# Expert blocks: Silu in place of Sigmoid and a product, the bias row spread one block ahead, and the first bias banks written earlier

## The reference, cut to what matters

```
logits = (hf @ router_w + router_b)
top_logits, top_idx = lax.top_k(logits, TOP_K)
gates = jax.nn.softmax(top_logits, axis=-1)
...
def expert_block(args):
    xb, e = args
    gu = xb @ w_gate_up[e] + b_gate_up[e]
    gate, up = jnp.split(gu, 2, axis=-1)
    gate = jnp.minimum(gate, SWIGLU_LIMIT)
    up = jnp.clip(up, -SWIGLU_LIMIT, SWIGLU_LIMIT)
    act = (up + 1.0) * gate * jax.nn.sigmoid(SWIGLU_ALPHA * gate)
    return act @ w_down[e] + b_down[e]
...
y_sorted = yb.reshape(n_rows, d)[dest] * gate_sorted[:, None]
out = jnp.zeros((n, d), h.dtype).at[tok_sorted].add(y_sorted)
```

## Time and profile before

| | us |
|---|---|
| median of 3 runs | 2066.52 |
| the 3 runs | 2066.52, 2068.47, 2065.49 |
| span of the profiled execution, first to last instruction | 2064.2 |
| granted TensorE clock, mean over the span | 0.997 of full speed |
| PE busy | 2018.9 (98%) |
| DVE busy | 1539.6 (75%) |
| ACT busy | 1189.2 (58%) |
| POOL busy | 494.7 (24%) |
| bytes moved by DMA | 521.92 MB |

### The profile page before, as it was taken

The page is one execution under the profiler, slowest core; times in us unless marked ns, Lnnn a source line. Parts: engine busy times, 40 slices in busy tenths (PEclk is TensorE's granted clock), DMA queues, the critical chain, the costliest instruction groups (busy, mean ns, idle before and its releaser), DMA issues.

```text
span 2064.2 us, 26261 instructions
## 1 busy us (share of the span) xinstructions
PE 2018.9 (98%) x9156; PEld 1601.7 (78%) x9156; DVE 1539.6 (75%) x1433; ACT 1189.2 (58%) x1182; POOL 494.7 (24%) x246
## 2 busy tenths in 40 slices
PE   8999999999999999999999999989999999999998
PEld 4865478888888888888888888858888878888887
DVE  5987499999999999999999999985684443333333
ACT  3132277878787878787878788854115632221222
POOL 0005325353434343434343434300000000000000
PEclk9999999999999999999999999999999999999999
DMA  6232599999999999999999999941131213222321
GB/s 228 92 143 89 207 394 407 392 397 378 392 381 391 382 389 380 385 377 390 382 386 386 385 385 383 386 150 69 63 107 70 82 41 113 102 102 83 121 82 41
DMA packets 79078, 521.92 MB, mean 253 GB/s; under 512 B 10368, under 2 KB 10896, under 8 KB 22160
## 3 DMA queue, kind: packets, MB, share of 16 engines
q1 hardware_dynamic: 66560, 484.14, 59.1%
q0 software_dynamic: 8912, 29.57, 5.7%
q10 hardware_dynamic: 3552, 7.46, 1.1%
HBM read 500.53 MB, written 18.60 MB: 251 GB/s over the span
## 4 chain that ended last, share of the span: by engine, by line
PE 84%; issue 5%; POOL 4%; DVE 3%; ACT 2%; DMA 2%; SPq 0%; POOLq 0%; DVEq 0%; ACTq 0%
PE bank L1141 24%; PE bank L1143 23%; PE bank L1142 23%; PE bank L1133 4%; POOL room L600 3%; PE bank L1482 1%; PE bank L1150 1%; ACT bank L842 1%; PE bank L1290 1%; DMA ring<-in_wmoe 1%; PE bank L1330 1%; PE bank L1179 1%; PE bank L1561 1%; PE bank L1542 1%; PE bank L1577 1%
## 5 line engine op out<-in xcount | busy, mean ns | idle before, releaser
L1897 DVE TENSOR_TENSOR ring_r<-ring,room_r 128x2048 fp32r<-128x2048 f32 x384 | 862.5, 2286 | 80.4 <-ACT room_r L774 80.4
L774 ACT ACTIVATE room_r<-ring 128x2048 fp32r<-128x2048 f32 x384 | 724.2, 1911 | 39.3 <-PE bank L1143 34.8
L1142 PE MATMUL bank<-ring_r,room_r 128*128 128x512 f32 x1744 | 679.2, 389 | 0.0
L1141 PE MATMUL bank<-room_r 128*128 128x512 f32 x1576 | 628.9, 399 | 15.8 <-ACT bank L842 13.0
L1143 PE MATMUL bank<-room_r 128*128 128x512 f32 x1568 | 611.8, 390 | 0.0
L1142 PEld LDWEIGHTS bank<-ring_r,room_r 128*128 128x128 f32 x1744 | 327.9, 188 | 66.9 <-issue 3.1
L1141 PEld LDWEIGHTS bank<-room_r 128*128 128x128 f32 x1576 | 295.9, 188 | 88.5 <-issue 29.2
L1143 PEld LDWEIGHTS bank<-room_r 128*128 128x128 f32 x1568 | 294.3, 188 | 63.0
L1141 PE MATMUL bank<-room_r,ring_r 128*128 128x512 f32 x520 | 203.5, 391 | 1.8 <-DVE ring_r L2059 0.9
L1143 PE MATMUL bank<-room_r,ring_r 128*128 128x512 f32 x512 | 199.3, 389 | 0.0
L604 POOL COPY idx_row<-places 96x1 uint32 (+1 forms) x32 | 106.9, 3340 | 267.3 <-DMA sum_rows<-room,idx_row 267.3
(11 more groups left out here) (292 smaller groups left out, 2290.0 us busy)
## 6 DMA issues: line engine op xcount, KB each, us to landing
ring<-in_wmoe SPq DMA_DIRECT2D x384, 1024.0 KB, 10.7
ring<-in_wf SPq DMA_DIRECT2D x33, 1024.0 KB, 4.8
ring<-in_wd SPq DMA_DIRECT2D x7, 2048.0 KB, 9.4
ring<-in_wp SPq DMA_DIRECT2D x14, 1024.0 KB, 4.8
ring<-in_wo SPq DMA_DIRECT2D x2, 2048.0 KB, 8.7
ring<-in_wd SPq DMA_DIRECT2D x2, 1024.0 KB, 9.3
room<-in_xtok ACTq DMA_DIRECT2D x1, 2048.0 KB, 12.6
h_rows<-room POOLq DMA_DIRECT2D x4, 512.0 KB, 3.0
```

Source lines behind the costliest of these rows:

```text
L774: act.activation(w_hi[pair(first, s_)], raw_w[ORDER[s_]], ACT.Copy)\
L1141: pe.matmul(out, x_hi, w_hi, start=start, stop=False, skip_group_check=True)
L1142: pe.matmul(out, x_hi, w_lo, start=False, stop=False, skip_group_check=True)
L1897: dve.tensor_tensor(w_lo[i], raw_w[i], w_hi[pair(first, s_)].bitcast(F32), ALU.subtract)\
```

## The change

Three edits in the expert part. First, ACT computes Silu of 1.702 times the gate bank and DVE's product L1952 is gone; the limit is scaled by 1.702, and the gates that the rows carry are multiplied by 1/1.702 once, before the loop. Second, the bias row of block b + 1 is loaded during the loads of block b (behind piece 3, or behind the last piece for block 0), and POOL spreads it in `block_pool(b)` when the gathered rows of block b + 1 have landed, ahead of the output of block b - 1. POOL then waits for the end of the broadcast, and the broadcast waits until both pairs of bias banks of block b are written. Third, ACT writes the first pair of bias banks straight behind the split of the rows and ahead of the split of the piece of step 1; they wait for the first activation of the block before (`act_ready`), no longer for `x_lo`. A later user of the same memory, in the second model block, gets a wait for the last broadcast.

```diff
-TOP_GATE = float(LIMIT / (1.0 + np.exp(-SW_ALPHA * LIMIT)))
+TOP_SILU = float(SW_ALPHA * LIMIT / (1.0 + np.exp(-SW_ALPHA * LIMIT)))
...
             def block_loads(b, first):
                 expert = sp.value_load(meta[0:1, bass.ts(b, 1)], min_val=0, max_val=E - 1)
-                if not first:
-                    sp.wait_ge(s["bias_spread"], b)
-                sp.dma_start(bias_row, a["bgu"][bass.ts(expert, 1), :]).then_inc(s["bias_in"], 16)
+                if first:
+                    sp.dma_start(bias_row, a["bgu"][bass.ts(expert, 1), :]).then_inc(s["bias_in"], 16)
                 for i in range(PIECES):
...
                     sp.dma_start(raw_w[i], a["wmoe"][bass.ts(expert, 1), i].rearrange("o p n -> (o p) n"))\
                       .then_inc(raw_in[i], 16)
+                    if i == (PIECES - 1 if first else 3):
+
+                        following = sp.value_load(meta[0:1, bass.ds(b + 1, 1)], min_val=0, max_val=E - 1)
+                        sp.wait_ge(s["bias_spread"], b + 1)
+                        sp.dma_start(bias_row, a["bgu"][bass.ts(following, 1), :]).then_inc(s["bias_in"], 16)
...
-            def spread_bias(b, first):
+            def spread_bias(b, first=False):
 
                 wait_counted("bias_in", b * 16 + 16)
                 if not first:
                     wait_counted("seeded", b * CHUNKS)
                 pool.partition_broadcast(bias_wide, bias_row).then_inc(s["bias_spread"], 1)
+                wait_counted("bias_spread", b + 1)
...
                 wait_counted("rows_in", b * 16 + 16)
-                if not first:
-                    spread_bias(b, first)
                 wait_counted("xt_ready", b + 1)
                 gather(b + 1)
+
+                wait_counted("rows_in", b * 16 + 32)
+                spread_bias(b + 1)
                 if not first:
                     rows_out(b - 1)
...
-            def sigmoids(b, c):
+            def silus(b, c):
 
                 act.wait_ge(s["gate_done"], b * CHUNKS + (c + 1))
-                act.activation(sig_sb[0:CAP, :], bank[2 * c][0:CAP, :], ACT.Sigmoid, scale=SW_ALPHA)\
-                   .then_inc(s["sig_done"], 1)
+                act.activation(silu_sb[0:CAP, :], bank[2 * c][0:CAP, :], ACT.Silu, scale=SW_ALPHA)\
+                   .then_inc(s["silu_done"], 1)
...
-                        act.wait_ge(s["x_lo"], b + 1)
+                        act.wait_ge(s["act_ready"], b * CHUNKS - 1)
...
                 split_hi(b, 0)
-                sigmoids(b - 1, 1)
+                silus(b - 1, 1)
                 gathered_hi(b)
+                seeds(b, 0)
                 split_hi(b, 1)
-                seeds(b, 0)
                 split_hi(b, 2)
...
-            step.mark(dve.tensor_copy(pairs[:, :].bitcast(F32).rearrange("p (i k o) -> p i k o", i=TT, k=TOPK)[:, :, :, 2],
-                                      gate[:, :, :]))
+            step.mark(dve.tensor_scalar(pairs[:, :].bitcast(F32).rearrange("p (i k o) -> p i k o", i=TT, k=TOPK)[:, :, :, 2],
+                                        gate[:, :, :], 1.0 / SW_ALPHA, None, ALU.mult))
...
                 own.mark(dve.tensor_scalar(up, bank[2 * c + 1][0:CAP, :], 1.0 - LIMIT, 1.0 + LIMIT, ALU.max, ALU.min))
-                dve.wait_ge(s["sig_done"], b * CHUNKS + (c + 1))
-                own(dve.tensor_tensor(sig, bank[2 * c][0:CAP, :], sig, ALU.mult))
-                dve.scalar_tensor_tensor(act_sb[c][0:CAP, :], sig, TOP_GATE, up, ALU.min, ALU.mult)\
+                dve.wait_ge(s["silu_done"], b * CHUNKS + (c + 1))
+                own.wait()
+                dve.scalar_tensor_tensor(act_sb[c][0:CAP, :], silu_sb[0:CAP, :], TOP_SILU, up, ALU.min, ALU.mult)\
                    .then_inc(s["act_ready"], 1)
...
             step.mark(dve.memset(AT, 0.0))
+
+            dve.wait_ge(s["bias_spread"], T + 1)
             for j in range(4):
```

More of the change, by code:

```diff
@@ L258, in build @@
         up_sb = v(5120, 512)
-        sig_sb = v(5632, 512)
+        silu_sb = v(5632, 512)
         act_sb = [v(6144, 512), v(6656, 512)]
@@ L361, in build @@
             idx_kept tok_kept rows_in bias_in bias_spread seeded hi_done lo_done used gate_done
-            sig_done act_ready xt_ready x_hi x_lo turned act_hi act_lo y_copied row_sel_ready sums_ready c2_in s2_ready x2_ready ss_ready
+            silu_done act_ready xt_ready x_hi x_lo turned act_hi act_lo y_copied row_sel_ready sums_ready c2_in s2_ready x2_ready ss_ready
             un_ready unT_ready uT_done_a uT_done_v p_ready p_evac hsig_ready rot_done fK_ready lv_ready lv_upd
@@ L854, in first_chunk @@
             def first_chunk(b, first=False):
-                sigmoids(b, 0)
+                silus(b, 0)
                 split_hi(b, 9, first)
@@ L890, in rest_act @@
             def rest_act(b):
-                sigmoids(last, 1)
+                silus(last, 1)
                 split_hi(b, 2, end=last)
@@ L1945, in activations @@
             def activations(b, c):
-                own = Steps(dve, s["moe_dve"], b * (2 * CHUNKS) + 2 * c)
-                up, sig = up_sb[0:CAP, :], sig_sb[0:CAP, :]
+                own = Steps(dve, s["moe_dve"], b * CHUNKS + c)
+                up = up_sb[0:CAP, :]
                 dve.wait_ge(s["used"], after(b, 5 + 4 * c))
                 own.mark(dve.tensor_scalar(up, bank[2 * c + 1][0:CAP, :], 1.0 - LIMIT, 1.0 + LIMIT, ALU.max, ALU.min))
-                dve.wait_ge(s["sig_done"], b * CHUNKS + (c + 1))
-                own(dve.tensor_tensor(sig, bank[2 * c][0:CAP, :], sig, ALU.mult))
-                dve.scalar_tensor_tensor(act_sb[c][0:CAP, :], sig, TOP_GATE, up, ALU.min, ALU.mult)\
+                dve.wait_ge(s["silu_done"], b * CHUNKS + (c + 1))
+                own.wait()
+                dve.scalar_tensor_tensor(act_sb[c][0:CAP, :], silu_sb[0:CAP, :], TOP_SILU, up, ALU.min, ALU.mult)\
                    .then_inc(s["act_ready"], 1)
```

## The result

The change makes the kernel slower by 0.5%, little but clear of noise: 2076.72 us (median of 4 runs, 2076.30 to 2076.79) against 2066.39 us for the kernel before, measured beside it (4 runs, 2065.49 to 2068.47). The ratio is 1.0049, 95% interval 1.0035 to 1.0064. The prediction was 2054.8, faster, range 2047 to 2070: wrong in direction, and outside its range. The rival that ended on the other side gave 2074.9.

A forecast was written before the change was run, and what follows sets the result against it. The prediction took PE to bound the kernel, with DVE close behind. Its terms, -17.1 - 1.6 + 1.0 + 3.0 + 3.0 = -11.7 us, gave a span of 2052.5 and a median of 2054.8, range 2047 to 2070.

The forecast's parts named there:

- The rival that ended on the other side: Broadcast let in between DVE's third and fourth splits in every block, +0.3 us a block, 2074.9 us; chance 0.15.
- it misses the gap: Broadcast too late for the pause before DVE's splits of steps 4 to 8: 0.1 us a block, +3.0; chance 0.55.
- The seam's -17.1: PE's lost time between row transposes and step 0 disappears: -0.57 us in each of blocks 2 to 31.
- Worth 0 by itself: Removing DVE's product L1952, 0.68 us twice a block, gains nothing, since PE does not wait for it in the loop.
- I take the upper end: Gathered rows land 10.5 us after the gather starts, from 8.5 to 10.5, so the broadcast is ready at about 883.4.
- It waits for the end of the run: Broadcast waits until DVE's splits of steps 4 to 8 end at 894.6, then holds DVE until 896.5.
- each keeps itself up: Catching or missing the pause before DVE's fourth split repeats from block to block; a late output delays the next gather.
- the 2047.8 of the sum: Time in us if the broadcast hardly holds DVE and the output also keeps its time; hardly held had chance 0.15.
- the 1.89: The time in us for which a broadcast on POOL holds DVE off, out of its 2.29.
- The late output at the end: After the last block, an output 6 to 7 us later makes PE wait for the sums: +3.0, bounds 2 and 5.
- the slower case: Broadcast let in before DVE's fourth split in every block: +0.3 us a block, block 1 adds -0.6; chance 0.15.
- The slower rival: Broadcast delays DVE's fourth split: 0.87 us lost for 0.57 gained a block, period 35.1, 2074.9 us; chance 0.15.

The follow-up runs named there:

- The two runs with the product in one half block: Kernel before with Silu, DVE's product put back in one half block only: first half 2065.43 us, second half 2049.38 us.
- the run behind step 4: Changed kernel with one more POOL wait, for ACT's split of step 4, ahead of the broadcast: 2083.55 us, ratio 1.0082.
- the run behind the activation: Changed kernel with the broadcast also waiting for DVE's activation of the first half of block b: 2053.70 us, ratio 0.9938.
- The mixed row: Changed kernel, spread row holding half of block b + 1's bias and half of block b's, spread ahead of the gather: 2048.47 us; with sigmoid and product 2054.78.

## Why the prediction was wrong

**The step that failed is "it misses the gap", the term of +3.0 (0.1 a block).** In 30 of 31 blocks the broadcast came into the gap, and each of these cost 0.93 in place of 0.1: 27.9 us. The seam's -17.1 came out; with it and the -0.3 of block 1 that is 10.5, and the span rose by 10.6. Three things led there: the landing time, the idea of what happens when the gap is missed, and a sum that was hardly on its own side. It had the broadcast ready at 883.4, and the run of five beginning at 883.49. By its own numbers, too, it was still in the gap, by 0.1, and "likeliest" did not follow.

**"Worth 0 by itself" (the product on DVE): wrong, by 16.1 us, though it hardly moved the sum,** since behind a closed seam it is worth 1.7. I looked for who waits for the product's result and found nobody. But the seam hung on POOL's broadcast, that on the copy ahead of it, and the copy on the end of DVE's run of splits; rows 7 showed the copy ending with that run, and the prediction used it for the other stall only. The run follows the multiply at once (splits of steps 9, 10, 11 and 0), so 0.68 less ahead of it ends it 0.5 earlier against PE (2.12 behind the transposes, where it was 2.66). The two runs with the product in one half block show that this place is what counts.

**"I take the upper end" (10.5 for the gather): wrong, by 1.4 to 1.6 us, and it chose the case.** Views of DMA and POOL of the kernel after, block 2 (in the block at 842 it was 8.9):

```profile
room<-h_rows,idx_tok POOLq DMA_INDIRECT x1, 9.1
```
```profile
315.84 0.97 POOL L595 DMA_INDIRECT room<-h_rows,idx_tok  x1 [0.82 <-POOL idx_tok L593]
```

The gather was issued where forecast, 3.5 behind the transposes, but its instruction takes 0.96 and not 2.79. The time from issue to landing in rows 9 held 1.8 us in which POOL's issue stood behind a split. A landing time carries what its issue waited for; moved to a free stretch, that part is gone. The fuller queue was real: from the end of the issue to the landing it was 8.5 - 2.8 = 5.7 in the block of rows 9 and is 8.9 - 1.0 = 7.9 now. But block 2, with its 10.5 - 2.8 = 7.7, already stood in such a queue, and taking the whole 10.5 counted the wait for the split as well. The broadcast was ready at 12.9 behind the transposes, not at 14.5.

**"It waits for the end of the run": wrong at this place.** It came from POOL's copies. With the broadcast asked for behind the start of the run the time is 2083.6, not 2054.8 (the run behind step 4). So the branch that was forecast did not arise even where the gap was missed, and "each keeps itself up" fell with it.

**Right: the seam and its 0.57** (closed in the kernel after; 2046.96 without the broadcast against the 2047.8 of the sum); **the 1.89** at gap and border alike, while the recorded end of the broadcast is 2.17 behind its letting-in, so the last 0.3 don't hold DVE. (The Trainium skill, SBUF — State Buffer, SBUF: two separate sides, has the pair of ports held "for the whole instruction"; these runs agree but for those 0.3, and the measurement decides.) **Right in size: the late output at the end** (3.0 against 3.52 in the run behind the activation), but in the changed kernel the output kept its time, and PE does not idle there. Right too were the duration of Silu (0.60 against 0.59 for the sigmoid) and the table load (none in the loop). Block 1 gained 0.31 of the 0.6 that the slower case had for it.

**The slower rival** was the case: a period of 35.1 against 35.14, 0.87 lost against 0.93, 2074.9 against 2076.7. It had 0.15. It had the mechanism as well as the number. The 10.5 that spoke against it was not taken apart.

## What to carry to other kernels

Where GpSimd and VectorE share a port, look for time that the former's instructions spend waiting inside their own recorded length (a copy of 0.17 us that takes 3), and follow that to VectorE's run: whatever VectorE does ahead of such a run is on GpSimd's path, even if nobody waits for its result. Place a broadcast where the next instructions of VectorE have more slack than the hold, and test it with one wait moved, since here the same broadcast costs 1.5 to 36.6 us by its place. Take each edit of a bundle by itself: Silu alone gave 16.1 of the 19.3 us that the change gains without its broadcast.

## What was not expected of the hardware

Whether a broadcast is let in at a border goes with how early DVE's next split was ready. I read all borders at which a single broadcast had been issued during a split and another split followed at once, in nine traces, and set the end of ACT's split that the next one reads against the border. In all 78 cases in which the broadcast got in, that input was ready 0.15 to 0.53 us before the border; in all 99 in which it did not, 0.57 to 2.76. The cases are not independent: 62 of the 78 are one border (steps 4 and 5) in two kernels. The mixed row has both kinds, 13 that got in at 0.52 to 0.53 and 12 that did not at 0.57 to 0.88. How early the broadcast was issued does not sort them (0.6 to 2.3 against 0.1 to 1.7). At the border of steps 4 and 5 it is 0.52 in every block, at the border of steps 11 and 0 it is 0.68 to 1.23 in all such cases but one, and that one got in. The second of two broadcasts in a row got in at the next border even with inputs ready up to 2.6 us before. No run moved the input alone, so that this is the cause is not shown, and why it should be is open.

An indirect DMA's issue on POOL also stands behind DVE's splits (2.7 to 2.8 us in place of 0.96). In the loop of the kernel before, every gather's issue from block 2 on ends 0.83 to 0.86 us behind the end of a split, and every output's 1.33 to 1.40 behind one.

The kernels with Silu alone (2050.4), with the broadcast ahead of the copies on top of it (2048.6) and with the mixed row (2048.5) beat both kernels. Their intervals overlap, so which of them is best is not told; the first is by far the smallest edit.
